# A float32 network on one core: memory attention and squared-relu fronts merged into their neighbours, output rows spread over the recurrence's waits

## The reference, cut to what matters

```
h = rmsnorm(x, g[0]);  y = even_mixer(h, ...)            # layer 0; layer 1: band attention
x = x + rmsnorm(y, g[1])
h = rmsnorm(x, g[2])
x = x + rmsnorm(memory_cross_attention(h, mem_n, w_q, w_kv, w_o), g[3])
h = rmsnorm(x, g[4])
x = x + rmsnorm(squared_relu_mlp(h, w1, w2), g[5])

def memory_cross_attention(h, mem_n, w_q, w_kv, w_o):    # 4 heads of 256, 256 memory rows
    q = h @ w_q;  k, v = mem_n @ w_kv
    p = softmax(q @ k.T * 256 ** -0.5)
    return (p @ v) @ w_o

def squared_relu_mlp(h, w1, w2):                         # width 4096
    a = relu(h @ w1)
    return (a * a) @ w2
```

## Time and profile before

| | |
|---|---|
| median of 3 runs | 1807.8 us |
| profiled execution | 1808.25 us, span 1806.3 us |
| PE busy | 1772.4 us (98%) |
| PEld busy | 1547.4 us (86%) |
| DVE busy | 1160.9 us (64%) |
| ACT busy | 868.8 us (48%) |
| POOL busy | 62.1 us (3%) |
| weight loads (q1) | 300.96 MB, 50.2% of 16 DMA engines |
| granted TensorE clock | 0.999 |

### The profile page before, as it was taken

One profiled execution on the slowest core, in us unless ns is written; L12 is line 12 of the kernel. 1 busy time (PEld: TensorE's weight loads), 2 busy tenths in 40 slices (PEclk: granted clock), 3 DMA queues, 4 the chain that ended last, 5 costly groups with the idle time before them and its releaser, 6 DMA issues.

```text
span 1806.3 us, 25833 instructions
## 1 busy us (share of the span) xinstructions
PE 1772.4 (98%) x10482; PEld 1547.4 (86%) x10482; DVE 1160.9 (64%) x1166; ACT 868.8 (48%) x1060; POOL 62.1 (3%) x102
## 2 busy tenths in 40 slices
PE   9999999999999999999999999999999999999998
PEld 7889988888988878888888899888888888788887
DVE  6665465557456465556666755667676666876665
ACT  7535455556455454555433466533353334553343
POOL 1000000000120000000000100000000000110000
PEclk9999999999999999999999999999999999999999
DMA  9526356556546345554556553565555555336552
GB/s 310 183 70 221 106 187 202 194 186 189 164 160 229 105 162 202 197 196 155 184 189 205 169 163 117 176 208 178 194 175 186 193 194 186 118 117 210 187 184 93
DMA packets 217157, 318.08 MB, mean 176 GB/s; under 512 B 5585, under 2 KB 179809, under 8 KB 217074
## 3 DMA queue, kind: packets, MB, share of 16 engines
q1 hardware_dynamic: 212274, 300.96, 50.2%
q0 software_dynamic: 4800, 15.94, 2.8%
HBM read 315.83 MB, written 1.05 MB: 175 GB/s over the span
## 4 chain that ended last, share of the span: by engine, by line
PE 93%; DVE 4%; ACT 2%; issue 0%; DMA 0%; SPq 0%; ACTq 0%; DVEq 0%
PE Y L1824 29%; PE C L1747 22%; PE C L1751 12%; PE Y L1780 9%; PE C L1780 5%; PE C L1792 4%; PE Y L1714 3%; DVE xn L1178 1%; DVE w_lo L1137 1%; ACT xn L669 1%; PE C L2023 1%; PE C L1996 1%; PE C L1878 1%; PE Y L2043 1%; PE C L2317 1%; PE C L2035 1%
## 5 line engine op out<-in xcount | busy, mean ns | idle before, releaser
L1137 DVE TENSOR_TENSOR w_lo<-raw,w_hi 128x2048 fp32r<-128x2048 f32 x282 | 645.7, 2291 | 321.0 <-ACT w_hi L654 320.5
L654 ACT ACTIVATE w_hi<-raw 128x2048 fp32r<-128x2048 f32 x282 | 538.2, 1910 | 247.2 <-PE Y L1824 163.9
L1747 PE MATMUL C<-at_hl,w_hi 128*128 128x512 f32 x1440 | 342.8, 390 | 0.0
L1747 PEld LDWEIGHTS C<-at_hl,w_hi 128*128 128x128 f32 x1440 | 267.9, 188 | 54.1
L1824 PE MATMUL Y<-w_hi,hid_h 128*128 128x512 f32 x696 | 216.7, 392 | 0.0
L1824 PE MATMUL Y<-w_lo,hid_h 128*128 128x512 f32 x696 | 215.0, 390 | 0.0
L1824 PE MATMUL Y<-w_hi,hid_l 128*128 128x512 f32 x696 | 214.6, 390 | 0.0
L1751 PEld LDWEIGHTS C<-at_hl,w_lo 128*128 128x128 f32 x1440 | 184.9, 191 | 7.2
L1751 PE MATMUL C<-at_hl,w_lo 128*128 128x256 f32 x1440 | 187.1, 283 | 0.0
L1824 PEld LDWEIGHTS Y<-w_lo,hid_h 128*128 128x128 f32 x696 | 130.7, 188 | 28.1
L1824 PEld LDWEIGHTS Y<-w_hi,hid_l 128*128 128x128 f32 x696 | 130.7, 188 | 27.9
(11 more groups left out here) (297 smaller groups left out, 2251.9 us busy)
## 6 DMA issues: line engine op xcount, KB each, us to landing
raw<-in_ffn_w_in SPq DMA_DIRECT2D x88, 1024.0 KB, 5.1
raw<-in_w_ff SPq DMA_DIRECT2D x64, 1024.0 KB, 5.6
raw<-in_ffn_w_out SPq DMA_DIRECT2D x44, 1024.0 KB, 4.9
raw<-in_w_mem_kv SPq DMA_DIRECT2D x16, 1024.0 KB, 5.7
raw<-in_w_qkv SPq DMA_DIRECT2D x12, 1024.0 KB, 5.5
raw<-in_sb_w_qkv SPq DMA_DIRECT2D x12, 1024.0 KB, 5.2
raw<-in_w_in_ab SPq DMA_DIRECT2D x8, 1024.0 KB, 9.8
raw<-in_w_mem_q SPq DMA_DIRECT2D x8, 1024.0 KB, 5.2
```

What stands on the lines that cost most here:

```text
L654: nc.scalar.activation(w_hi[:, n % RING, :], raw[:, n % RAW, :], ACT.Copy).then_inc(hi_split, 1)
L1137: V.tensor_tensor(w_lo[:, n % RING, :], raw[:, n % RAW, :], w_hi[:, n % RING, :].bitcast(f32), ALU.subtract).then_inc(lo_split, 1)
L1747: mm(tiles(C[:, 2 * pair + i, :], 2), wh[:, k, i * P:(i + 1) * P], hl[:, k, :, :], start=k == 0, stop=False)
```

## The change

`cols` and `softmax` become one stage, `mem_att`. TensorE does query chunks 0 and 1, the scores of head 0, chunk 2, the scores of head 1, chunk 3, and then turns, scores and contexts alternate. Scores go to banks 2 and 3 of Y (`mem_bank`). On ScalarE and VectorE the steps of the softmax stand among the last `hi` and `lo` of the stage.

In the recurrence, row chunks 0 and 1 are cut by block, and chunk 0's block 0 by half, and stand in front of the last level's scores, in front of the output, and around the two turns. The `hi` and `lo` of row chunks 2 and 3 move forward on ScalarE and VectorE.

In layer 0's front both blocks are turned before it, and VectorE splits the tokens before `lo` of the next chunk. In layer 1's front, half of pair chunk n + 1 is done by block (`pair_block`), block 0 in place of the four matmuls on zeros, block 1 behind the front; its `w_lo` half (`pair_lo`) stands behind the turn. The front's bank is now C 0 in both layers, the turned tokens go to Y.

```diff
-            net += [("cols", mem_q(l), q_to), ("softmax", 4), ("rows", "w_mem_o", l)]
+            net += [("mem_att", mem_q(l), q_to), ("rows", "w_mem_o", l)]
...
# ScalarE, mem_att
+                hi(n + 2)
+                copied(0, specs, to, at)
+                hi(n + 3)
+                copied(1, specs, to, at)
+                hi(n + 4)
+                mem_exps(0)
+                copied(2, specs, to, at)
+                hi(n + 5)
+                mem_exps(1)
+                copied(3, specs, to, at)
+                mem_out(0)
+                mem_out(1)
+                mem_exps(2)
+                mem_exps(3)
+                contexts(0, at, "mem")
+                mem_out(2)
...
# ScalarE, even
+                hi(at.chunk + AHEAD)
                 act.wait_ge(rec_ready, 1)
...
-                hi(at.chunk + AHEAD)
+                hi(at.chunk + 1 + AHEAD)
                 for b in range(TB):
                     act.wait_ge(rec_turned, b + 1)
...
-                hi(at.chunk + 1 + AHEAD)
...
# VectorE, meanwhile
                 for i in range(n):
+                    if n == 2 and i == 1:
+                        norm_lo("at", then, Y)
                     lo(at.chunk + i + AHEAD)
...
# VectorE, mem_att
+                lo(n + 2)
+                lo(n + 3)
+                mem_max(0)
+                lo(n + 4)
+                mem_shares(0)
+                mem_max(1)
+                lo(n + 5)
+                mem_shares(1)
+                mem_max(2)
+                mem_max(3)
+                mem_shares(2)
+                mem_shares(3)
+                for i in range(4):
+                    contexts(i, at, "mem")
...
# VectorE, even
+                lo(at.chunk + AHEAD)
                 dve.wait_ge(rec_squared, 1)
...
-                lo(at.chunk + AHEAD)
                 for b in range(TB):
                     dve.wait_ge(rec_hi, b + 1)
...
-                lo(at.chunk + 1 + AHEAD)
+                    if b == 0:
+                        lo(at.chunk + 1 + AHEAD)
...
# TensorE
+            def pair_block(n, hl, pair, b):
+
+                w = w_hi[:, n % RING, :].rearrange("p (k c) -> p k c", k=KT)
+                pe.wait_ge(hi_split, n + 1)
+                tokens = slice(b * P, (b + 1) * P)
+                for i in range(2):
+                    for k in range(KT):
+                        mm(tiles(C[:, 2 * pair + i, :], 2)[:, :, tokens], w[:, k, i * P:(i + 1) * P], hl[:, k, :, tokens],
+                           start=b == 0 and k == 0, stop=False)
...
-                front_one(n, front_bank(same), at, Y if same else C, not same)
-                pair_chunk(n + 1, at_hl, 1, some=[0])
-                front_turn(at)
-                pair_chunk(n + 1, at_hl, 1, some=[1])
+                split = at.turned - 4
+                if same:
+                    for b in range(TB):
+                        last = front_part(n, at_h, at_l, b, front_bank, split, range(3))
+                    last.then_inc(chunk_done, 1)
+                    pair_chunk(n + 1, at_hl, 1, some=[0])
+                    front_turn(at)
+                    pair_chunk(n + 1, at_hl, 1, some=[1])
+                else:
+                    front_part(n, at_h, at_l, 0, front_bank, split, range(3))
+                    pair_block(n + 1, at_hl, 1, 0)
+                    turn_block(1, at.xn, Y)
+                    front_part(n, at_h, at_l, 1, front_bank, split, range(3)).then_inc(chunk_done, 1)
+                    pair_block(n + 1, at_hl, 1, 1)
+                    front_turn(at)
+                    pair_lo(n + 1, at_hl, 1).then_inc(chunk_done, 1)
...
# TensorE, even
+                    if l == 1 + len(LEVELS):
+                        pe.wait_ge(level_exp, 1 + len(LEVELS))
+                        out_part(at, 0, [0], [0])
...
+                out_part(at, 0, [0], [1])
                 pe.wait_ge(level_used, 2 + len(LEVELS))
-                pe.wait_ge(level_exp, 1 + len(LEVELS))
...
-                rows(at, range(2))
-                for b in range(TB):
+                def rec_turn(b):
...
+                out_part(at, 0, [1])
+                out_part(at, 1, [0])
+                rec_turn(0)
+                out_part(at, 1, [1])
+                rec_turn(1)
+                for b in range(TB):
+                    pe.wait_ge(rec_lo, b + 1)
+                    for r in (2, 3):
+                        out_part(at, r, [b])
```

More of the change, by code:

```diff
@@ L399, in counts @@
                 return dict(x=2)
[L400 to L401 removed]
+            if s[0] == "mem_att":
+                return dict(chunk=4, copied=4, head=4, ctx=4)
             if s[0] == "even_cols":
@@ L784, in meanwhile @@
                     norm_hi("at", then, Y)
-            def cols(specs, to, at):
-                for i in range(len(specs)):
-                    hi(at.chunk + i + AHEAD)
-                    copied(i, specs, to, at)
             def kv_cols_(to, at):
@@ new lines, in mem_scores @@
+                def mem_scores(i):
+                    pe.wait_ge(cols_copied, at.copied + i + 1)
+                    if i >= 2:
+                        pe.wait_ge(probs_ready, h0 + i - 1)
+                    for b in range(TB):
+                        for k in range(2):
+                            last = mm(mem_bank(i)[:, b * S:(b + 1) * S], qT[:, 2 * i + k, b * P:(b + 1) * P],
+                                      mem_kT[:, 2 * i + k, :], start=k == 0, stop=k == 1)
+                    last.then_inc(scores_ready, 1)
@@ new lines, in mem_context @@
+                def mem_context(k):
+                    pe.wait_ge(probs_copied, h0 + k + 1)
+                    for half in range(2):
+                        for kb in range(2):
+                            first = k * S + half * P
+                            last = mm(ctx_bank("mem", k)[:, half * S:(half + 1) * S], vt[:, kb, first:first + P],
+                                      pT[k % 2][:, kb * S:(kb + 1) * S], start=kb == 0, stop=kb == 1)
+                    last.then_inc(probs_used, 1)
```

230 lines of the change are left out of this document (108 added, 122 removed).

## The result

The changed kernel takes 1796.36 us (median of 6 runs, 1795.08 to 1796.8) against 1807.38 us for the kernel before beside it (6 runs, 1806.42 to 1808.2): ratio 0.9939, 95% interval 0.9926 to 0.9952. It is faster by 11.0 us. The forecast stood on 1807.8 us, three runs of the kernel before; its six runs beside the changed kernel gave 1807.38, and this accounts for 0.42 of the 2.24 us between 1798.6 and 1796.36. The profiled execution took 1796.12 us, its span is 1794.2.

The account below looks back on a forecast made before the run. TensorE's own pace bounds the loops, so only its holes can give time: 4.4 + 2.6 + 1.35 + 1.2 = 9.55 us, less 0.35, net 9.2, from 1807.8 to 1798.6 us; own range 1797.0 to 1800.5, widened to 1796.8 to 1802.4.

Parts of the forecast that it names:

- Front of layer 0: Layer 0's front, turns to pair chunk: both turns first and VectorE splitting before `lo` gain 1.35 us, bounds 0.9 and 1.5.
- Changes of kind: Some four new changes between kinds of matmul, outside holes, at about 0.1 us each: 0.35 us deducted from the sum.
- Memory attention: Memory attention in both layers: holes of 1.5 us close, gain 1.3 us each, 2.6 in both; bounds 0.8 and 1.5 each.
- The hole at head 2's turn: Memory attention: TensorE waits 0.1 to 0.3 us at head 2's turn, its shares standing behind head 3's maximum on DVE.
- Fronts: Fronts of layer 0 and layer 1: gains of 1.35 us and 1.2 us.
- The hole before `down(0)`: Layer 1's front: a new wait of 0.5 us opens before `down(0)`, on the split of the hidden block.
- pieces cost like wholes: Rival, layer 1's front: 2 x 128 columns take 0.229 us, not 0.120; gain 5.7 us, 1802.1 us; chance 0.07.
- The recurrence: Recurrence: old holes of 5.04 us close, new ones of 0.61 open; gain 4.4 us, bounds 3.0 and 5.0.
- The early splits' slack: Recurrence: with `hi` and `lo` moved forward, `lo` of row chunk 3 is done 2 us before it is wanted.
- the fillers push the chain: Rival, every place: fillers delay the dependent chains, half the gain at each, 4.6 us, 1803.2 us; chance 0.12.
- Given back to the loads: Rival, later stages: weights bound them, so the gain becomes waits on `w_lo`, 1807.8 us; chance 0.03.
- The loop falls out of step: Rival, loop behind layer 1's front: its 30 chunks each wait for DVE, at 0.5 us each 1813.6 us; chance 0.02.

Follow-up runs that it names:

- x1: Changed kernel with VectorE's `lo` of the second weight chunk back ahead of `norm_lo` after two-chunk memory-key projections: 1797.47 us, ratio 0.9945 to the kernel before.
- x7: Kernel before with only VectorE's `norm_lo` moved ahead of the second `lo` after two-chunk memory-key projections: 1805.12 us, ratio 0.9989 to the kernel before.
- x8: Changed kernel with memory attention's old order on all three engines, scores still in their new banks: 1797.68 us, ratio 0.9945 to the kernel before.
- x6: Changed kernel with the hidden block's high part ahead of ScalarE's next `hi`, and head 2's shares ahead of head 3's maximum on VectorE: 1795.29 us.
- x5: Changed kernel without the recurrence's fillers, early `hi` and `lo` kept, both turns together: 1803.28 us, ratio 0.9980 to the kernel before.
- x10: x5 with VectorE's second `lo` (row chunk 3) behind both subtractions of the normed blocks: 1799.56 us, ratio 0.9960 to the kernel before.
- x2: Kernel before with only the recurrence's part of the change: 1802.33 us, ratio 0.9974 to the kernel before.
- x11: Changed kernel with six matmuls on zeros at its start in place of four: 1795.14 us, ratio 0.9933 to the kernel before.
- x9: x6 with six matmuls on zeros at its start in place of four: 1794.15 us, ratio 0.9930 to the kernel before.

## Why the prediction was right in kind and short in size

By the starts the change gives 11.4 us, and 0.65 more lie in the start's scatter. The net sum was 9.2. With every bound of its terms at the best and nothing deducted (5.0 + 3.0 + 1.5 + 1.2 = 10.7) it would still have been short of 11.4: the bounds could not hold a place that was not in the sum. The 2.2 us between are five differences:

- **The failed step: the sum was made over four places (the recurrence, memory attention, the two fronts), and one edit serves a fifth, which was put at nothing without a reason.** `norm_lo` ahead of `lo` was costed in "Front of layer 0" alone, but `meanwhile` with two chunks also stands ahead of band attention in layer 1, and TensorE waited 1.25 us there. x1 and x7 give and take 1.05 us at that place, with nothing else changed. The wait was in the trace; its row named `w_lo`, which the change does not bring sooner, and the prediction does not ask what was queued behind `w_lo`. This is half of the error, 1.05 us.
- **Changes of kind, 0.35 deducted, next to nothing measured.** The first pair behind small fp32 matmuls is 0.1 to 0.2 us longer, and in memory attention the group ahead of it is shorter by as much: eight scores among the query chunks take 1.54 us to the next start where 8 x 0.216 are 1.73. Only one side had been counted. (In the recurrence the 16 scores ahead of a filler are only 0.05 us shorter, 1.70 from 102.10 to 103.81, for 0.10 behind them.)
- **Memory attention, 1.3 each forecast, 1.54 measured.** The same short end: of the 15.62 us of work, 16 contexts take 3.27 and not 3.46, so the holes were 1.67 and not 1.48. With 0.14 left, 1.53. Banks and order share it as 0.9 to 0.65 (x8). The hole at head 2's turn, forecast 0.1 to 0.3, is there, and x6 closes it.
- **Fronts, 1.35 and 1.2 forecast, 1.51 and 1.30 measured.** Layer 0's is the deduction for kinds again. In layer 1 the 1.30 us are 1.57 less 0.14, since the turn came late (0.1 forecast), and less the 0.13 at the loop's first matmuls. The hole before `down(0)` is 0.33, not 0.5. The forecast had kept the old end of the hidden block's split, but ScalarE's copy before it had waited 0.16 us for the turns; now the turns are there and the copy starts at 652.37, 1.80 behind `hi`'s start at 650.57 where it was 2.06, and the split is done at 653.67. The new form cost 0.120 us per matmul, so the rival by which pieces cost like wholes falls. With pieces of 128 adjacent floats at that pace, the Trainium skill's rule that non-contiguous PSUM access slows matmuls (SBUF — State Buffer, Door 1: The DMA port swizzle) does not show here.
- **The recurrence, 4.4 forecast, 4.49 measured**, with the holes where they were put: none before the last scores, 0.2 before the output (0.34 forecast), 0.2 before the first turn (0.27), none behind the turns. The early splits' slack, given as 2 us, is there only because the turns come one by one (x5, x10).

Of the rivals, "the fillers push the chain" would have shown as holes of half the old size; they are 0.4 together of 5.04. "Given back to the loads" falls with x2, where 4.50 stays 4.50 to the end. "The loop falls out of step" does not show: the 0.13 us arise in the first matmuls behind the hole before `down(0)`, the rest of the loop keeps its pace, and x6, which closes the hole, takes them away.

## What to carry to other kernels

Before a sum is made of an edit to a helper, list every call of the helper in the program and read the idle time at each: the gain sat in a call the diff's title does not name. Read a printed releaser against its own end time; if it had been done well before the wait ended (0.70 us here, where the true one ended 0.10 before), look at what is queued behind it on that engine. Where filler work splits a pair of dependent steps, the order on the other engines belongs to it: take the filler away alone and the result may be worse than before, as x5 shows: 8.5 us lost where the fillers are worth 3.95, and 4.0 us behind the kernel before.

## What was not expected of the hardware

- A pause of 3.9 us of TensorE, with a granted clock of 0.78 in it, is followed by twelve matmuls at the pace of 0.50 (the window of 4.4 us above, and on to 128.0) and costs 2.4 us more than itself (x5). A pause of 1.7 us at the same place (x10, and before) leaves it at 1.00.
- At the kernel's start the first turns and matmuls run at up to twice their later time (0.217 against 0.12 us for 256 columns in the kernel before, 13.12 to 14.86). The windows print a granted clock of 1.00 there, but the trace has no record of the clock before 14.70, so that 1.00 says nothing; the pace is read from the starts. Where the slow stretch ends varies between executions of the kernels with four zero matmuls from 10.24 to 15.36 us and moves everything behind by up to 2.3 us; single runs of the kernel before lie 1.9 us apart (1806.2 to 1808.05). What decides that time stays open: x11's and x9's runs only hint that being busy up to the first turns helps.
